# p2 as three fp32r products instead of one plain fp32 product, with a12 split into a high and a low part, in 33 of 41 groups of the SwiGLU layers

## The chip, the core and the metric

One core of one Trainium2 chip runs the whole program. The metric is the device time of one execution in microseconds (us). TensorE (PE) multiplies, VectorE (DVE), ScalarE (ACT) and GpSimd (POOL) work on elements, and SyncE (SP) issues the loads of the weights.

## The reference, cut to what matters

Two layers, each of them x += 0.5 SwiGLU(norm x); x += Mixer(norm x); x += 0.5 SwiGLU(norm x), on 528 positions (16 learned ones and 512 given ones) of 1024 features, in float32. The four SwiGLU stages are what the change touches:

```
def swiglu(h, w_gate, w_up, w_down):
    return (jax.nn.silu(h @ w_gate) * (h @ w_up)) @ w_down
h = h + 0.5 * swiglu(rmsnorm(h, g[0]), ffn_w_gate[layer, 0], ffn_w_up[layer, 0], ffn_w_down[layer, 0])
```

w_gate and w_up are 1024 x 2816 (22 tiles of 128 columns each), w_down is 2816 x 1024. The last stage needs the 512 given positions alone.

## The kernel before

**Tiles and precision.** Positions lie along the free axis, features along the 128 partitions. A float32 number is split into a high part, rounded to the type fp32r (ACT writes it, into `wh` for weights, `fh` and `hs` for activations), and a low part, the rest (DVE subtracts, into `wl`, `fl`, `hs`). A product of 128x128 weights with a block of columns is then three matmuls in fp32r: high by high, high weights by low activations, low weights by high activations. One product, p2, is not split: it multiplies the float32 `raw` and `ff` as they are, one matmul call for each 128x128 block, and each call shows in the trace as two matmul instructions.

**Passes and groups.** Each of the four stages q is two passes p (10 and 12 hidden tiles of 128; the first six tiles of the first stage are done in the ordinary way). A pass works through groups g of two hidden tiles, a and b, with the gate's and the up projection's weights side by side: 2, 6, 5, 6, 5, 6, 5 and 6 groups, 41 in all. Within a group the 2x2 blocks (input features in two halves, positions in two halves of 264, or 256 in the last stage) are multiplied by Strassen's method in Winograd's form: seven products p1 to p7, for the gate (n = 2g) and for the up projection (n = 2g+1). Each product has four 128x128 blocks, so it is 12 fp32r matmuls, and p2 is 8 records of the plain kind. The weights' quarters a11, a21, a22, a12 of 128x1024 are loaded by SP into the four slots of `raw`; DVE and ACT make the sums s1 to s4 and the parts of them. p2 is a12 by B21 (the second feature half, first positions half), added to p1 in the same bank of PSUM; s4 is a12 + s2.

**The order.** Each engine follows an order written out by hand in the program, and waits on semaphores. In the leading group of a pass (`leads(g)`) PE does p1 p5 of the gate, p1 p5 of up, p2, p2, p6, p6, p7, p7, p4, p3, p3, p4. In each later one, here with a dash for up: p1, p7, (p3' of the group before), p6, (p4' of the group before), p2, p5, p1', p7', p3, p6', p4, p2', p5'. The parts in brackets are there from the pass's third group on, which is called a steady group here; the pass's second group is without them. In a steady group DVE does c22, `low_s2`, `low_s1`, then `up_a_out` and `sum_s4` (both wait for p3' of the group before), `hidden_low` and further work. ACT does `high_s1`, `p1_copy`, `hidden_high`, `u_copy`, `high_s4` and further work. p5 adds to a bank that `u_copy` fills with p6's result. SP loads a11 of the next group when `sum_s4` is done, a12 of the next group when both p2 are done.

After its groups each pass does its part of the down projection (`down`): 8 output tiles, each from two chunks of `w_down` of 5 or 6 blocks (640 or 768 columns) in slots 1024 wide; the conversions of a chunk cover all 1024 columns. During the last output tiles ACT and DVE prepare the quarters of the next pass's leading group.

GpSimd clears `ss` seven times, copies and multiplies in the two mixers, and does nothing in the groups.

Of the kernel before, what the change touches and what calls it, by code (L numbers as in the profile page):

```python
# [5 lines left out]
F32R = mybir.dt.float32r  # L6
# [79 lines left out]
def leads(g):  # L86

    return g == GROUP[PASS_OF[g]][0]


def leading(g):
# [93 lines left out]
def trunk(nc, x_dram, gains, w_gu, w_dn, ev_in, ev_out, od_in, od_out, conv_w, sinks, rel_bias, gate_b, pool_w,  # L185
          pool_scale, ident_in, onehot_in, causal_in, sel_in, out):
    table_dram = nc.dram_tensor("bias_table", [P, 8, TABLE], F32, kind="Internal").ap()
    with ExitStack() as ctx:
        def sb(name, shape, dt=F32):
            return ctx.enter_context(nc.sbuf_tensor(name, shape, dt))  # L190
# [3 lines left out]


        x = sb("x", [P, KT, L])
        raw = sb("raw", [P, RING, CW])
        wh_at = (nc.sbuf_base + 31) // 32 * 32
        wh = sb("wh", [P, 6, CW], F32R)
        wl_at = (nc.sbuf_base + 31) // 32 * 32  # L200
# [4 lines left out]
        up = sb("up", [P, L])  # L205
        ss = sb("ss", [P, L])
        sq = sb("sq", [P, L])
        spare_at = (nc.sbuf_base + 31) // 32 * 32
        spare = sb("spare", [P, 3, L + 2])
        sb("spare_end", [P, 8])  # L210
        ss_parts = nc.alloc_sbuf_tensor_at("ss_parts", [P, 2, L], F32R, offset=spare_at + (4 * (L + 2) + 31) // 32 * 32)
        gate2, up2 = spare[:, 0, 2:2 + L], spare[:, 1, 0:L]
        ones_r = sb("ones_r", [P, P], F32R)
# [149 lines left out]
        form_ready, first_ready, u_added = sem("form_ready"), sem("first_ready"), sem("u_added")  # L363
        down_front, down_back, down_scaled = sem("down_front"), sem("down_back"), sem("down_scaled")
        table_kept = sem("table_kept")

        block = ctx.enter_context(nc.Block())

# [36 lines left out]
            return ss_parts[:, part, :]  # L405
        def gain(v, m):
            return g_sb[:, bass.ds(KT * v + m, 1)]

        def raw_quarter(kind, g):
            return raw[:, raw_slot(kind, g), :]  # L410
# [135 lines left out]
        def _(act):  # L546
            def high(n):

                slot = n % RING
                act.wait_ge(raw_in[slot], RAW_COUNT[n])  # L550
                for (q, p), (first, count) in GROUP.items():
                    at = n - CHUNK[down_name(q, p)]
                    if 0 <= at < RING:
                        form = (p6_done, p5_done, p3_done, p4_done)[at]
                        act.wait_ge(form, 2 * (first + count))
                if n >= RING:
                    act.wait_ge(chunk_done, n - RING + 1)
                act.activation(wh[:, slot, :], raw[:, slot, :], ACT.Copy).then_inc(wh_ready, 1)  # L558

            def next_high(n):  # L560
                if n + RING < CHUNKS:
# [52 lines left out]
            def high_a22(g):  # L614
                ring_done("a22", g)
                act.wait_ge(raw_in[raw_slot("a22", g)], RAW_COUNT["a22", g])
                if g:
                    act.wait_ge(p4_done, 2 * g)
                act.activation(wh[:, form_slot("a22", g), :], raw_quarter("a22", g), ACT.Copy).then_inc(a22_high, 1)

            def split_x(v, m, to):
                act.activation(to[:, m, 0, :], x[:, m, :], ACT.Copy, scale=gain(v, m)).then_inc(xh_ready, 1)
# [82 lines left out]
            def groups(q, p):  # L705
                real = q == 3
                lo = N_META if real else 0
                first, count = GROUP[q, p]
                end = first + count
                for g in range(first, end):  # L710
                    if g > first:
                        high_s1(g)
                        p1_copy(2 * g, real)
                    if g == first:
                        p1_copy(2 * g + 1, real)
                        high_a22(g)
                        high_a11(g + 1)
                        if q and not p:
                            pair_root(V_FFN[q], real)
                            warm(ACT.Silu)  # L720
                    if g > first:
                        hidden_high(g - 1, real, 0)
                        u_copy(2 * g, real)
                        high_s4(g)
                        high_a22(g)
                        hidden_high(g - 1, real, 1)
                    if g == first:
                        u_negative(2 * g, real)
                        if (q, p) == (0, 0):
                            act.wait_ge(hl_ready, STD_F)  # L730
                        u_negative(2 * g + 1, real)
                    p7_copy(2 * g, real)
                    if g > first:
                        u_negative(2 * g, real)
                        p1_copy(2 * g + 1, real)
                    if g > first and g + 1 < end:
                        high_a11(g + 1)
                    if g + 1 < end:
                        high_s3(g + 1)
                    if g > first:  # L740
                        u_copy(2 * g + 1, real)
                        act.wait_ge(hl_ready, FT * q + group_f(g))
                    p7_copy(2 * g + 1, real)
                    if g > first:
                        u_negative(2 * g + 1, real)
                    if g + 1 == end:
# [12 lines left out]
                hidden_high(end - 1, real, 1)  # L759
                high(n + 2)  # L760
                high(n + 3)
# [13 lines left out]
            def down(q, p):  # L775
# [8 lines left out]
                for i in range(KT):  # L784
# [27 lines left out]
                    if g is not None and i == 7:  # L812
                        p1_copy(2 * g, real)
                        high_s4(g)
                    if x_next:
                        x_high(q + 1, i, False)
                    if g is not None and i == 5:
# [251 lines left out]
        def _(pool):  # L1069
# [8 lines left out]
            def clear_ss(v):  # L1078
# [6 lines left out]
            clear_ss(1)  # L1085

            pool.memset(zbuf[:, 0:2], 0.0).then_inc(pool_step, 1)
            steps[0] += 1
# [19 lines left out]
                    pool.tensor_tensor(zbuf[:, 2:2 + L], conv_c[:, :], conv_x[:, :], ALU.mult).then_inc(z_ready, 1)  # L1108
            clear_ss(2)
            clear_ss(3)  # L1110
            clear_ss(4)

            for s in range(OD_TILES):
                if s == 0:
# [27 lines left out]
            pool.wait_ge(yd_l, 4)  # L1142
            clear_ss(5)
            clear_ss(6)
            pool.wait_ge(x_gained, KT - 1)
            for h, (a, b) in enumerate(ENDS):
                pool.wait_ge(rms_ready, 7 + h)
# [5 lines left out]
        def _(dve):  # L1153
# [8 lines left out]
            def low(n):  # L1162

                slot = n % RING
                dve.wait_ge(wh_ready, n + 1)
                dve.tensor_tensor(wl[:, slot, :], raw[:, slot, :], f32(wh[:, slot, :]), ALU.subtract).then_inc(wl_ready, 1)  # L1166

            def low_gates(n):

# [80 lines left out]
            def low_a22(g):  # L1250
                slot = form_slot("a22", g)
                dve.wait_ge(a22_high, g + 1)
                dve.tensor_tensor(wl[:, slot, :], raw_quarter("a22", g), f32(wh[:, slot, :]), ALU.subtract).then_inc(a22_low, 1)

            def add_square(v, i, real=False):

# [157 lines left out]
            def groups(q, p):  # L1414
# [4 lines left out]
                for g in range(first, end):  # L1419
# [20 lines left out]
                        c22(2 * g - 1, real)  # L1440
                    low_s2(g)
                    low_s1(g)
                    up_a_out(g - 1, real)
                    sum_s4(g)
                    hidden_low(g - 1, real, 0)
                    if g > first + 1:
                        c21(2 * g - 1, real)
# [14 lines left out]
                        low(n)  # L1462
                    c21(2 * g, real)
                    gate_b_scale(g, real)
                c22(2 * end - 1, real)
                low(n + 1)
                up_a_out(end - 1, real)
# [7 lines left out]
            def down(q, p):  # L1475
# [6 lines left out]
                for i, m in enumerate(order):  # L1482
# [30 lines left out]
                        low_s1(g)  # L1513
                    if g is not None and i == 7:
                        low_s4(g)
                    if x_next:
                        x_low(q + 1, i, False)
                    if g is not None and i == 5:
# [417 lines left out]
        def _(pe):  # L1936
# [116 lines left out]
            def p2(n, real, q=None):  # L2053
                s, g = n % 2, n // 2
                w, slot = width(real), raw_slot("a12", g)
                pe.wait_ge(raw_in[slot], RAW_COUNT["a12", g])
                pe.wait_ge(p1_copied, n + 1)
# [28 lines left out]
            def ffn(q, p):  # L2086
# [4 lines left out]
                for g in range(first, end):  # L2091
# [428 lines left out]
```

## Time and profile before

| | |
|---|---|
| median of 3 runs | 1844.7 us (1844.44 to 1845.2) |
| the profiled execution: device time | 1844.85 us |
| its span, first to last instruction | 1843.0 us |
| mean granted TensorE clock | 0.998 of 2.4 GHz |
| PE busy | 1822.8 us, 99% of the span |
| DVE busy | 1347.9 us, 73% |
| ACT busy | 867.3 us, 47% |
| POOL busy | 53.2 us, 3% |
| PE's share of the chain that ended last | 94% |

Busy time is the time in which an engine has an instruction under way. Matmuls overlap in the records: one lasts longer than the step from its start to the next start, and the steps are what add up to the time. In the chain that ended last, each piece is given its step.

### The profile page before, as it was taken

The page shows a single profiled execution, that of the slowest core. Times are in us where ns is not written, and L with a number is a line of the kernel's source. Part 1 is how long each engine was busy: PE and PEld are TensorE (multiplying, and loading weights), DVE is VectorE, ACT ScalarE, POOL GpSimd, SP SyncE. Part 2 cuts the span into 40 slices and gives each one's busy share as a digit, 9 for nine tenths or more (in the row PEclk, how much of TensorE's full clock was granted, in tenths as well). Part 3 has the DMA queues.
Part 4 walks back from the last instruction along what each step waited for, and adds up shares of the span by engine and source line. Part 5 has one row for each costly group of instructions (what it writes and reads, how often), then busy time and mean ns, then how long its engine had stood idle before and what let it go on. Part 6 is the DMA issues. An engine that isn't in the chain of part 4 may idle for free.

```text
span 1843.0 us, 32078 instructions
## 1 busy us (share of the span) xinstructions
PE 1822.8 (99%) x13192; PEld 1724.7 (94%) x13192; DVE 1347.9 (73%) x1777; ACT 867.3 (47%) x1367; POOL 53.2 (3%) x68
## 2 busy tenths in 40 slices
PE   8999999999999999999999999999999999999997
PEld 8999999999999999999999999999998899889986
DVE  7767787657678867886888678865656798678855
ACT  7443554434445543554555335544422555435542
POOL 0000000000000000000000000000123000000000
PEclk9999999999999999999999999999999999999999
DMA  5255233341222333233223332333212222332331
GB/s 177 88 90 115 94 114 101 106 134 59 69 70 81 104 93 114 81 104 103 81 92 106 94 99 92 109 104 118 92 58 69 69 82 102 101 105 93 109 105 62
DMA packets 81104, 176.83 MB, mean 96 GB/s; under 512 B 7292, under 2 KB 12700, under 8 KB 80960
## 3 DMA queue, kind: packets, MB, share of 16 engines
q1 hardware_dynamic: 80544, 174.49, 30.6%
q8 instruction: 106, 1.74, 0.4%
q14 instruction: 38, 0.31, 0.1%
q10 hardware_dynamic: 416, 0.29, 0.0%
HBM read 171.35 MB, written 3.41 MB: 95 GB/s over the span
## 4 chain that ended last, share of the span: by engine, by line
PE 94%; DVE 2%; ACT 1%; issue 1%; DMA 0%; SPq 0%; DVEq 0%; ACTq 0%
PE psum L1944 25%; PE psum L2014 13%; PE psum L2016 12%; PE psum L2017 12%; PE psum L2061 8%; PE psum L1954 7%; PE psum L1953 4%; PE psum L1957 4%; PE psum L1952 4%; PE psum L1956 3%; ACT wh L608 0%; DMA rb_sb<-in_rel_bias 0%; DVE rms L1319 0%; PE psum L2228 0%; DVE wl L1166 0%
## 5 line engine op out<-in xcount | busy, mean ns | idle before, releaser
L2014 PE MATMUL psum<-fh,wh 128*128 128x264 f32 (+1 forms) x1968 | 572.0, 291 | 2.5 <-ACT psum L673 2.5
L2017 PE MATMUL psum<-fh,wl 128*128 128x264 f32 (+1 forms) x1968 | 557.2, 283 | 0.0
L2016 PE MATMUL psum<-fl,wh 128*128 128x264 f32 (+1 forms) x1968 | 556.9, 283 | 0.0
L2014 PEld LDWEIGHTS psum<-fh,wh 128*128 128x128 f32 x1968 | 371.1, 189 | 6.4 <-issue 4.0
L2016 PEld LDWEIGHTS psum<-fl,wh 128*128 128x128 f32 x1968 | 371.0, 189 | 2.4
L2017 PEld LDWEIGHTS psum<-fh,wl 128*128 128x128 f32 x1968 | 369.9, 188 | 0.0
L1166 DVE TENSOR_TENSOR wl<-raw,wh 128x1024 fp32r<-128x1024 f32 x193 | 237.4, 1238 | 95.7 <-ACT wh L558 95.2
L558 ACT ACTIVATE wh<-raw 128x1024 fp32r<-128x1024 f32 x194 | 203.2, 1055 | 210.8 <-PE psum L1944 165.6
L1944 PE MATMUL psum<-xs,wh 128*128 128x264 f32 (+1 forms) x1504 | 267.3, 297 | 5.8 <-DVE xs L1269 4.2
L1944 PEld LDWEIGHTS psum<-xs,wh 128*128 128x128 f32 x1504 | 213.6, 189 | 16.5 <-issue 5.3
L1954 PE MATMUL psum<-hs,wh 128*128 128x512 f32 x528 | 206.6, 391 | 0.0
L1944 PE MATMUL psum<-hs,wh 128*128 128x512 f32 (+2 forms) x760 | 192.3, 349 | 0.0
L1944 PE MATMUL psum<-xs,wl 128*128 128x264 f32 (+1 forms) x736 | 161.9, 294 | 0.0
L2061 PE MATMUL psum<-ff,raw 128*128 128x264 f32 (+1 forms) x656 | 156.7, 384 | 0.0
L1953 PE MATMUL psum<-hs,wh 128*128 128x272 f32 x528 | 152.5, 289 | 0.0
L1957 PE MATMUL psum<-hs,wl 128*128 128x272 f32 x528 | 151.3, 287 | 0.0
L1952 PE MATMUL psum<-hs,wh 128*128 128x272 f32 x528 | 150.6, 285 | 0.0
L1956 PE MATMUL psum<-hs,wl 128*128 128x256 f32 x528 | 147.6, 280 | 0.0
L1944 PEld LDWEIGHTS psum<-hs,wh 128*128 128x128 f32 x760 | 128.4, 188 | 20.0
L2061 PEld LDWEIGHTS psum<-ff,raw 128*128 128x128 f32 x656 | 119.1, 189 | 15.8
L1944 PE MATMUL psum<-hs,wl 128*128 128x512 f32 (+2 forms) x380 | 122.8, 351 | 0.0
L1957 PEld LDWEIGHTS psum<-hs,wl 128*128 128x128 f32 x528 | 99.1, 188 | 22.0
(298 smaller groups left out, 2707.4 us busy)
## 6 DMA issues: line engine op xcount, KB each, us to landing
raw<-in_w_gate_up SPq DMA_DIRECT2D x175, 512.0 KB, 3.6
raw<-in_w_down SPq DMA_DIRECT2D x64, 384.0 KB, 3.2
raw<-in_w_down SPq DMA_DIRECT2D x64, 320.0 KB, 3.0
raw<-in_od_in SPq DMA_DIRECT2D x21, 512.0 KB, 3.5
raw<-in_ev_in SPq DMA_DIRECT2D x18, 512.0 KB, 3.5
raw<-in_ev_out SPq DMA_DIRECT2D x8, 512.0 KB, 3.5
raw<-in_od_out SPq DMA_DIRECT2D x8, 512.0 KB, 3.4
x<-in_x_t SPq DMA_DIRECT2D x8, 264.0 KB, 5.6
```

Of the source, the lines that this page charges most:

```text
L558: act.activation(wh[:, slot, :], raw[:, slot, :], ACT.Copy).then_inc(wh_ready, 1)
L1166: dve.tensor_tensor(wl[:, slot, :], raw[:, slot, :], f32(wh[:, slot, :]), ALU.subtract).then_inc(wl_ready, 1)
L1944: last = pe.matmul(dst, weights[:, slot, w], both[:, at, part, tok], start=start and p == 0, stop=stop and p == len(steps) - 1)
L1952: pe.matmul(a, wh[:, slot, w], both[:, k, 0, 0:FRONT], start=start, stop=False)
L1953: pe.matmul(a, wh[:, slot, w], both[:, k, 1, 0:FRONT], start=False, stop=False)
L1954: pe.matmul(psum[:, 2 * acc_at + 1, :].rearrange("p (h t) -> p h t", h=2), wh[:, slot, w], both[:, k, :, b], start=start, stop=False, skip ...
L1956: pe.matmul(back(acc_at, 0), wl[:, slot, w], both[:, k, 0, b], start=False, stop=stop, skip_group_check=True)
L1957: return pe.matmul(a, wl[:, slot, w], both[:, k, 0, 0:FRONT], start=False, stop=stop)
L2014: pe.matmul(psum[:, bank, 0:w], wh[:, slot, cols], high_x, start=start and j == 0, stop=False, skip_group_check=True)
L2016: pe.matmul(psum[:, bank, 0:w], wh[:, slot, cols], low_x, start=False, stop=False, skip_group_check=True)
L2017: last = pe.matmul(psum[:, bank, 0:w], wl[:, slot, cols], high_x, start=False, stop=j == 3, skip_group_check=True)
L2061: last = pe.matmul(psum[:, 4 * s, 0:w], raw[:, slot, 512 * s + P * j:512 * s + P * (j + 1)], ff[:, B21, j, 0:w], start=False, stop=j == 3, ...
```

## The change

p2 is split like the others in every group but the first two of each p = 0 pass: 41 - 8 = 33 groups by the program's own rule `plain(g)`. (The change was described as 35 groups, 31 of them with GpSimd; the program's rules give 33 and 29.) For it:

- ACT rounds a12 to fp32r (`high_a12`) into memory taken from `spare`, `sq` and `up`.
- The low part is written over a12 in `raw`, by GpSimd in the 29 groups that do not lead a pass, by DVE in the 4 leading groups of the p = 1 passes. It waits for `sum_s4`, which still reads a12.
- B21 is split once for each stage: ACT and DVE (`high_b21`, `low_b21`) write into `fl`.
- DVE's `sum_s4` is moved ahead of `up_a_out` in the steady groups.
- PE's order changes in the second group of each p = 1 pass: p1, p7, p6, p5, p1', p7', p2, p3, p6', p4, p2', p5'.
- The conversions of the down projection's chunks cover only the columns in use.

The `low_a12` and `groups` shown with `pool` are GpSimd's; DVE's `low_a12` subtracts in the same way.

```diff
+def plain(g):
+    q, p = PASS_OF[g]
+    return p == 0 and g < GROUP[q, p][0] + 2
+def parted(g):
+    return sum(not plain(h) for h in range(g + 1))
...
+            def high_a12(g):
+                q, p = PASS_OF[g]
+                act.wait_ge(raw_in[raw_slot("a12", g)], RAW_COUNT["a12", g])
+                act.wait_ge(p2_done, 2 * g)
...
+                act.activation(a12_in(g)[:, :], raw_quarter("a12", g), ACT.Copy).then_inc(a12_split, 1)
+            def high_b21(q, real):
+                act.wait_ge(t_ready, 4 * q + 4)
+                act.activation(fl[:, B12, :, 0:w], ff[:, B21, :, 0:w], ACT.Copy).then_inc(b21_split, 1)
...
                     if g > first:
+                        if not plain(g):
+                            high_a12(g)
                         hidden_high(g - 1, real, 0)
                         u_copy(2 * g, real)
                         high_s4(g)
...
+            def low_a12(g):
+                pool.wait_ge(a12_split, 2 * parted(g) - 1)
+                pool.wait_ge(s4_sum, g + 1)
+                pool.tensor_tensor(raw_low[:, raw_slot("a12", g), :], raw_quarter("a12", g), f32(a12_in(g)[:, :]),
+                                   ALU.subtract).then_inc(a12_split, 1)
+            def groups(q, p):
+                first, count = GROUP[q, p]
+                for g in range(first + 1, first + count):
+                    if not plain(g):
+                        low_a12(g)
...
+                w = chunk_cols(n)
+                dve.tensor_tensor(wl[:, slot, 0:w], raw[:, slot, 0:w], f32(wh[:, slot, 0:w]), ALU.subtract).then_inc(wl_ready, 1)
...
                     low_s2(g)
                     low_s1(g)
-                    up_a_out(g - 1, real)
+                    if g == first + 1:
+                        up_a_out(g - 1, real)
                     sum_s4(g)
+                    if g > first + 1:
+                        up_a_out(g - 1, real)
                     hidden_low(g - 1, real, 0)
...
+                    if q and not p and g == first + 1:
+                        low_b21(q, real)
...
                     if g is not None and i == 7:
                         low_s4(g)
+                        if not p:
+                            low_a12(g)
...
             def p2(n, real, q=None):
+                pe.wait_ge(p1_copied, n + 1)
+                if not plain(g):
+                    pe.wait_ge(b21_split, 2 * PASS_OF[g][0] + 2)
+                    pe.wait_ge(a12_split, 2 * parted(g))
+                    for j in range(4):
+                        cols = slice(512 * s + P * j, 512 * s + P * (j + 1))
+                        high_x, low_x = fl[:, B12, j, 0:w], fl[:, B21, j, 0:w]
+                        pe.matmul(psum[:, 4 * s, 0:w], a12_in(g)[:, cols], high_x, start=False, stop=False, skip_group_check=True)
+                        pe.matmul(psum[:, 4 * s, 0:w], a12_in(g)[:, cols], low_x, start=False, stop=False, skip_group_check=True)
+                        last = pe.matmul(psum[:, 4 * s, 0:w], raw_low[:, slot, cols], high_x, start=False, stop=j == 3,
+                                         skip_group_check=True)
+                    last.then_inc(p2_done, 1)
+                    return
...
+                    if p and g == first + 1:
+                        p6(n, real)
+                        p5(n, real)
+                        p1(n + 1, real)
+                        p7(n + 1, real)
+                        p2(n, real)
+                        p3(n, real)
+                        p6(n + 1, real)
+                        p4(n, real)
+                        p2(n + 1, real)
+                        p5(n + 1, real)
+                        continue
```

## Rows read from the trace of the kernel before

**Rows 1.** The page: busy time by engine, and the plain p2 among the groups.

```profile
PE 1822.8 (99%) x13192; PEld 1724.7 (94%) x13192; DVE 1347.9 (73%) x1777; ACT 867.3 (47%) x1367; POOL 53.2 (3%) x68
...
L2061 PE MATMUL psum<-ff,raw 128*128 128x264 f32 (+1 forms) x656 | 156.7, 384 | 0.0
...
raw<-in_w_gate_up SPq DMA_DIRECT2D x175, 512.0 KB, 3.6
```

**Rows 2.** The waits of PE: total us, times, longest.

```profile
PE psum L2014 <- ACT psum L673: 2.5, 8, 0.3
```

**Rows 3.** The chain that ended last, 723 to 790 us: start, us, engine, line.

```profile
730.11 3.56 PE psum L2061 x16
...
750.24 1.78 PE psum L2061 x8
...
760.75 1.78 PE psum L2061 x8
...
771.26 1.78 PE psum L2061 x8
```

**Rows 4.** The same chain in the last stage, 256 columns wide.

```profile
1646.01 3.45 PE psum L2061 x16
...
1696.48 1.73 PE psum L2061 x8
1706.75 1.73 PE psum L2061 x8
```

**Rows 5.** Timeline of DVE, a steady group that began at 764.0 us.

```profile
768.37 0.71 DVE L1389 TENSOR_TENSOR up<-psum,gate 128x528 f32<-128x528 f32 x1 [1.10 <-PE psum L2017]
768.99 1.22 DVE L1243 TENSOR_TENSOR ws<-raw 128x1024 f32<-128x1024 f32 x1
...
777.35 1.23 DVE L1185 TENSOR_TENSOR wl<-raw,wh 128x1024 fp32r<-128x1024 f32 x1 [1.19 <-ACT wh L583]
```

**Rows 6.** Timeline of ACT and of SP's queue, the same group.

```profile
765.92 0.37 ACT L673 ACTIVATE psum<-psum 128x264 f32<-128x264 f32 x1
...
769.11 0.65 ACT L703 ACTIVATE hs<-up 128x528 fp32r<-128x528 f32 x1 [2.82 <-DVE up L1389]
```
```profile
762.61 21.38 SPq L456 DMA_DIRECT2D raw<-in_w_gate_up  x5
```

**Rows 7.** Timeline of DVE and GpSimd in the odd mixer.

```profile
1328.68 0.71 DVE L1324 TENSOR_TENSOR gate<-psum,rms 128x528 f32<-128x528 f32 x1 [2.13 <-PE psum L1944]
1329.47 1.07 POOL L1134 TENSOR_TENSOR spare<-gate 128x527 f32<-128x527 f32 x1 [0.47 <-DVE gate L1324]
1329.83 1.79 DVE L1166 TENSOR_TENSOR wl<-raw,wh 128x1024 fp32r<-128x1024 f32 x1 [0.45 <-ACT wh L558]
```

**Rows 8.** GpSimd's subtraction and its smallest multiplication, by line: ns min/median/max.

```profile
L1140 POOL TENSOR_TENSOR up<-up,gate x2: 1283/1284/1286, 1333.1 to 1402.4; 128x512 f32<-128x512 f32 x2
```
```profile
L1149 POOL TENSOR_TENSOR x<-x,rms x4: 717/798/964, 1831.7 to 1838.4; 128x256 f32<-128x256 f32 x4
```

**Rows 9.** Timeline, PE's restart after a wait for ACT.

```profile
747.94 0.28 PE L2017 MATMUL psum<-fh,wl 128*128 128x264 f32 x1
748.01 0.37 ACT L673 ACTIVATE psum<-psum 128x264 f32<-128x264 f32 x1
...
748.52 0.36 PE L2014 MATMUL psum<-fh,wh 128*128 128x264 f32 x1 [0.31 <-ACT psum L673]
...
748.72 0.28 PE L2016 MATMUL psum<-fl,wh 128*128 128x264 f32 x1
```

**Rows 10.** Timelines of leading groups: ACT, DVE, and DVE in the last stage.

```profile
727.56 1.06 ACT L612 ACTIVATE wh<-ws 128x1024 fp32r<-128x1024 f32 x1 [1.40 <-DVE ws L1243]
```
```profile
728.65 1.23 DVE L1248 TENSOR_TENSOR wl<-ws,wh 128x1024 fp32r<-128x1024 f32 x1 [1.12 <-ACT wh L612]
```
```profile
1644.08 1.23 DVE L1248 TENSOR_TENSOR wl<-ws,wh 128x1024 fp32r<-128x1024 f32 x1 [1.13 <-ACT wh L612]
```

**Rows 11.** Timeline of ACT in the second group of a p = 1 pass.

```profile
750.01 0.65 ACT L703 ACTIVATE hs<-up 128x528 fp32r<-128x528 f32 x1 [1.63 <-DVE up L1389]
750.57 0.37 ACT L680 ACTIVATE psum<-psum 128x264 f32<-128x264 f32 x1
```

More of the change, by code:

```diff
@@ L88, in leads, with chunk_cols @@
     return g == GROUP[PASS_OF[g]][0]
+def chunk_cols(n):
+    for q in range(4):
+        for p in range(2):
+            if CHUNK[down_name(q, p)] <= n < CHUNK[down_name(q, p)] + COUNT[down_name(q, p)]:
+                return PASS_F[p] // 2 * P
+    return CW
+def plain(g):
[3 more added lines that the diff above has]
+    return sum(not plain(h) for h in range(g + 1))
 def leading(g):
@@ L196, in trunk @@
         x = sb("x", [P, KT, L])
+        raw_at = (nc.sbuf_base + 31) // 32 * 32
         raw = sb("raw", [P, RING, CW])
+        raw_low = nc.alloc_sbuf_tensor_at("raw_low", [P, RING, CW], F32R, offset=raw_at)
         wh_at = (nc.sbuf_base + 31) // 32 * 32
@@ L210, in trunk @@
         sb("spare_end", [P, 8])
+        sq_at = (nc.sbuf_base + 31) // 32 * 32
+        sq = sb("sq", [P, L])
+        up = sb("up", [P, L])
+        high_12 = nc.alloc_sbuf_tensor_at("high_12", [P, CW], F32R, offset=spare_at + (8 * (L + 2) + 31) // 32 * 32)
+        first_12 = nc.alloc_sbuf_tensor_at("first_12", [P, CW], F32R, offset=sq_at)
         ss_parts = nc.alloc_sbuf_tensor_at("ss_parts", [P, 2, L], F32R, offset=spare_at + (4 * (L + 2) + 31) // 32 * 32)
@@ L365, in trunk @@
         table_kept = sem("table_kept")
+        a12_split, b21_split = sem("a12_split"), sem("b21_split")
         block = ctx.enter_context(nc.Block())
@@ L407, in gain, with a12_in @@
             return g_sb[:, bass.ds(KT * v + m, 1)]
+        def a12_in(g):
+            return first_12 if leads(g) else high_12
         def raw_quarter(kind, g):
@@ L557, in high @@
                     act.wait_ge(chunk_done, n - RING + 1)
-                act.activation(wh[:, slot, :], raw[:, slot, :], ACT.Copy).then_inc(wh_ready, 1)
+                w = chunk_cols(n)
+                act.activation(wh[:, slot, 0:w], raw[:, slot, 0:w], ACT.Copy).then_inc(wh_ready, 1)
             def next_high(n):
@@ L745, in groups @@
                         u_negative(2 * g + 1, real)
+                    if q and not p and g == first + 1:
+                        high_b21(q, real)
                     if g + 1 == end:
@@ L814, in down @@
                         high_s4(g)
+                        if not p:
+                            high_a12(g)
+                    if (q, p) == (0, 0) and i == 1:
+                        high_b21(0, False)
                     if x_next:
@@ L1082, in clear_ss @@
                 pool.wait_ge(ss_zero, v + 1)
+            def low_a12(g):
[8 more added lines that the diff above has]
+                        low_a12(g)
             clear_ss(0)
             clear_ss(1)
+            groups(0, 1)
             pool.memset(zbuf[:, 0:2], 0.0).then_inc(pool_step, 1)
@@ L1110, in _ @@
             clear_ss(3)
+            groups(1, 0)
+            groups(1, 1)
             clear_ss(4)
+            groups(2, 0)
+            groups(2, 1)
             for s in range(OD_TILES):
@@ L1144, in _ @@
             clear_ss(6)
+            groups(3, 0)
+            groups(3, 1)
             pool.wait_ge(x_gained, KT - 1)
@@ L1165, in low @@
                 dve.wait_ge(wh_ready, n + 1)
-                dve.tensor_tensor(wl[:, slot, :], raw[:, slot, :], f32(wh[:, slot, :]), ALU.subtract).then_inc(wl_ready, 1)
+                w = chunk_cols(n)
+                dve.tensor_tensor(wl[:, slot, 0:w], raw[:, slot, 0:w], f32(wh[:, slot, 0:w]), ALU.subtract).then_inc(wl_ready, 1)
             def low_gates(n):
@@ L1253, in low_a22, with low_a12, low_b21 @@
                 dve.tensor_tensor(wl[:, slot, :], raw_quarter("a22", g), f32(wh[:, slot, :]), ALU.subtract).then_inc(a22_low, 1)
+            def low_a12(g):
+                dve.wait_ge(a12_split, 2 * parted(g) - 1)
+                dve.tensor_tensor(raw_low[:, raw_slot("a12", g), :], raw_quarter("a12", g), f32(a12_in(g)[:, :]),
+                                  ALU.subtract).then_inc(a12_split, 1)
+            def low_b21(q, real):
+                w = width(real)
+                dve.wait_ge(b21_split, 2 * q + 1)
+                dve.wait_ge(p2_done, 2 * GROUP[q, 0][0] + 4)
+                dve.tensor_tensor(fl[:, B21, :, 0:w], ff[:, B21, :, 0:w], f32(fl[:, B12, :, 0:w]), ALU.subtract).then_inc(b21_split, 1)
             def add_square(v, i, real=False):
@@ L1464, in groups @@
                     gate_b_scale(g, real)
+                    if q and not p and g == first + 1:
+                        low_b21(q, real)
                 c22(2 * end - 1, real)
@@ L1515, in down @@
                         low_s4(g)
+                        if not p:
+                            low_a12(g)
+                    if (q, p) == (0, 0) and i == 2:
+                        low_b21(0, False)
                     if x_next:
```

10 lines of the change are left out of this document (7 added, 3 removed).

## The prediction

> **What bounds the kernel now.** I read the page's busy times first: PE has an instruction under way in 99% of the span, DVE in 73%, and GpSimd in 3% [rows 1]. Then the waits of PE: in the groups the only one is for a copy of ACT's, 8 times and 2.5 us in all [rows 2]. So the groups are paced by PE's own steps, and two things can move the time there: fewer or cheaper steps, and waits that are new.
>
> The chain that ended last gives the steps. A plain p2 is 8 records and 1.78 us with 264 columns [rows 3], 1.73 us with 256 [rows 4]. Between the end of one p2 (762.53) and the start of the next (771.26) lie six split products: 8.73 / 6 = 1.455 us for one [rows 3]. With 256 columns it is (10.27 - 1.73) / 6 = 1.423 us [rows 4].
>
> **What the change gives.** A split p2 has the same 12 matmuls as any other product, so I price it at 1.455 and 1.423 us. 33 groups have two p2 each. 24 of them are in the first three stages: 48 x (1.78 - 1.455) = 15.6 us. 9 are in the last: 18 x (1.73 - 1.423) = 5.5 us. The gain is 21.1 us, all of it on the path that bounds.
>
> **The new wait in the steady groups.** There are 25 with GpSimd: 18 with 264 columns (4 in the first stage's second pass, 3 + 4 in each of the next two) and 7 with 256. Before, p2 needed only a12 in its slot. Now it needs a chain that begins when p3' of the group before ends, because `sum_s4` waits for that, and GpSimd overwrites what `sum_s4` reads. Step by step, from the moment PE leaves p3':
>
> - DVE starts 0.02 us later: p3' ends two products before p2, at 771.26 - 2.91 = 768.35, and DVE's next instruction starts at 768.37 after 1.10 us of idling [rows 3, 5]. That instruction is `up_a_out` now; `sum_s4`, behind it at 768.99, is the first one after the change. It takes 1.22 us [rows 5].
> - GpSimd starts 0.08 us after DVE has ended: 1328.68 + 0.71 = 1329.39, against 1329.47 [rows 7].
> - Its subtraction of 128x1024 is nowhere in this trace. The nearest row is the same operation with 512 columns, 1284 ns; the smallest, undisturbed instruction with 256 took 717 ns [rows 8]. The line through both gives 1284 + 2 x 567 = 2418 ns. From below I take the addition of 527 columns, 1.07 us [rows 7], scaled by 1024/527: 2.08 us. From above, twice 1284: 2.57 us. I take 2.40, near the line, since it rests on the same operation.
> - PE restarts 0.22 us after the event: ACT ended at 748.38, and the second matmul of the product started at 748.72, which is one step of 0.12 after an effective start of 748.60 [rows 9].
>
> The Trainium skill ("GPSIMD Engine Reference", section "Performance versus the Vector engine") gives 4497 ns for a two-input fp32 operation on 2048 columns and calls about 2.6 cycles for an element the floor. Half of it would be 2.25 us, an estimate from that page; by it the sum below would be 3.8 us smaller. The rows with 512 columns are a little slower than that, and I go by the rows.
>
> The chain is 0.02 + 1.22 + 0.08 + 2.40 + 0.22 = 3.94 us. What covers it is p6 and p4' on PE, 2.91 us, or 2.85 with 256 columns. So p2 starts 1.03 or 1.09 us late: 18 x 1.03 + 7 x 1.09 = 26.1 us. PE executes in order, so nothing fills that time.
>
> ACT's part of the split does not gate: `p1_copy` ends at 766.3, the a12 load is issued at 762.61 and lands some 3.6 us later, at 766.2 [rows 1, 6], so `high_a12` is over by 767.4, two us before `sum_s4`. It stands ahead of `hidden_high`, which started at 769.11 after 2.82 us of idling and now waits for the moved `up_a_out` [rows 6]; `u_copy` follows at about 771, and p5 needs it only after p2.
>
> **The leading groups of the p = 1 passes.** PE reaches p2 at 730.11 [rows 3]. ACT ends `high_s4` at 728.62 and `high_a12` at 729.6; DVE ends `low_s4` at 729.88, and its `low_a12` at 1.14 us later, the step of two such instructions [rows 10]: about 731.0. With 0.22 for the restart p2 starts at 731.2, 1.1 us late. The groups of three stages lie alike: 3.4 us. In the last stage `low_s4` ends at 1645.31, `low_a12` at 1646.45, and p2 was due at 1646.01 [rows 4, 10]: 0.66 us. Together 4.0 us; bounds 0 (if the split can come earlier) and 6.
>
> **The second groups of the p = 1 passes.** Their new order puts p5 straight behind p6, and p5 adds to the bank that `u_copy` fills from p6. Until now p2 covered that copy. p6 ends where p2 began, at 750.24; the copy ran from 750.57, behind `hidden_high`, to 750.94 [rows 3, 11]. With 0.22 for the restart p5 starts at 751.16: 0.92 us, four times, 3.7 us. GpSimd is in time there: p2 comes three products later, at about 755.5, and `sum_s4` is over by 751.2. What it may cost beyond that is c22 arriving late behind the held-up work of DVE: 0 to 1 us, taken as 0.
>
> **What costs nothing.** 33 roundings of a12 on ACT are hidden by its idle time (47% busy). B21's split is about one more instruction each on ACT and DVE, in each stage: in the second group of a p = 0 pass it comes just ahead of c22 and `low_s2`, and DVE idles 1.10 us right before `up_a_out` in that stretch [rows 5]. If that cover were gone it would cost up to 1.2 us three times. The narrower conversions take work from DVE and ACT during the down projections, while PE is busy anyway [rows 1], so I give them nothing. SP's load of a11 is released by `sum_s4` 0.6 us earlier in relation to p3', that of a12 as before.
>
> DVE loses time too while GpSimd works. A DVE instruction with two SBUF inputs that started at 1329.83, beside GpSimd's of 1329.47 to 1330.54, took 1.79 us and not 1.22, as if it had waited to its end [rows 7]. Here `hidden_low` will wait so, about 1 us. The cover is the 1.19 us for which DVE idled before `low_a11` [rows 5], and two us more in which the next group's forms are ahead of PE. The Trainium skill ("SBUF — State Buffer", section "SBUF: two separate sides") calls the shared port pair an exclusive lock held for the whole instruction; the rows agree as far as one pair can.
>
> **The sum.** -21.1 + 26.1 + 4.0 + 3.7 = +12.7 us. The profiled execution took 1844.85 us (0.15 above the median), so 1857.5 there and 1857.4 against the median of 1844.7: 0.7% slower. The point of balance is a GpSimd instruction of 2.40 - 12.7 / 25 = 1.89 us, below my lower bound; at 2.08 the sum is +4.7, at 2.57 it is +17.
>
> **The rivals.**
>
> 1. GpSimd's chain doesn't hold PE up. For it: the stall hangs on an instruction that this trace does not show. Against it: the instruction would have to end within 1.37 us, and half the columns take 1.28. With only the leading and second groups' waits the time is 1844.7 - 21.1 + 7.7 = 1831; with none at all 1824. It decides as soon as GpSimd takes clearly under 1.89 us, or if the wait for p3' comes earlier than I read it. Chance 0.20.
> 2. Stall and gain cancel: GpSimd at 1.9 to 2.0 us, or at 2.08 with the leading and second groups' waits half hidden (+0.8). 1841 to 1848. Chance 0.12.
> 3. GpSimd also waits for DVE. An instruction of DVE's with two SBUF inputs gets the port first and GpSimd starts behind it, 0.6 to 1.2 us later. Against it: behind `sum_s4` comes `up_a_out`, which reads PSUM, and after it ACT must first finish `hidden_high`. The time is 1857 + 25 x 0.6 = 1872 or more. Chance 0.08.
> 4. My forecast, 1848 to 1866: chance 0.60.
>
> **Range and chances.** From case 4's bounds I go down through the balance and half of rival 1, and a little up: 1831 to 1868. Within 0.2% (3.7 us, about what a measurement of this kernel can tell from no change) 0.11. Faster 0.23: rival 1 and a part of 2. Slower 0.66.
>
> **What the profile after would show.** PE's waits would name a new row, p2's first matmul waiting for GpSimd's subtraction, about 25 times and about 1 us each (by the record some 0.2 less). GpSimd's instruction lasts about 2.4 us. In the chain GpSimd and `sum_s4` have a share of 25 x 3.6 us, about 5%, where PE's falls. The step from one p2 to the next in a steady stretch grows from 10.51 us by about 0.2 on the mean. p2 shows 12 steps of 0.12 us. I am wrong if GpSimd's instruction is under 1.9 us, if `sum_s4` starts before p3' has ended, or if PE's busy share stays at 99%.

## The result, and the profile after

The changed kernel takes 1868.0 us (median of 4 runs, 1867.81 to 1868.86) against 1844.95 us, a ratio of 1.0126 (95% interval 1.0112 to 1.0139): 23 us slower. Forecast were 12.7 us, 1857.4 us, with a range that ended at 1868, which the measured 1868.01 us just misses. The direction was right, and so were most of the places where time is lost; the forecast loss is little more than half of the measured one.

The page of the changed kernel, against [rows 1]. TensorE (PE) has fallen from 99% to 97% of the span:

```profile
span 1866.1 us, 32745 instructions
...
PE 1812.2 (97%) x13456; PEld 1723.9 (92%) x13456; DVE 1348.1 (72%) x1785; ACT 863.0 (46%) x1404; POOL 123.3 (7%) x97
...
PE 82%; DVE 8%; POOL 3%; issue 2%; ACT 2%; DMA 2%; SPq 0%; DVEq 0%; POOLq 0%; ACTq 0%
...
L1143 POOL TENSOR_TENSOR raw_low<-raw,high 128x1024 fp32r<-128x1024 f32 x29 | 70.2, 2422 | 1002.2 <-DVE ws L1319 1002.2
```

PE's share of the chain that ended last went from 94% to 82%, and GpSimd's subtraction (L1143), 2.42 us each, stands in it with DVE's `sum_s4` (L1319). The waits of PE, where [rows 2] stood alone among the groups before (a wait under 0.15 us is not in this list):

```profile
PE psum L2160 <- POOL raw_low L1143: 27.0, 25, 1.3
PE psum L2160 <- DVE raw_low L1333: 3.7, 4, 1.1
PE psum L2111 <- ACT psum L728: 3.4, 4, 0.9
PE psum L2111 <- ACT psum L721: 2.5, 8, 0.3
...
PE psum L2111 <- DVE spare L1468: 1.5, 3, 0.8
```

The first is p2 waiting for GpSimd, 25 times: one for each steady group. Its recorded mean is 1.08 us; the time lost is larger, as the group below shows. The second is p2 in the four leading groups, the third p5 behind `u_copy` in the four second groups. The last one, c22 coming late, is new too; the prediction named it and took it as 0. A steady group, by the timelines of PE, DVE and POOL; before, DVE did `up_a_out` first [rows 5]:

```profile
797.41 0.28 PE L2114 MATMUL psum<-fh,wl 128*128 128x264 f32 x1
797.53 0.28 PE L2111 MATMUL psum<-fh,wh 128*128 128x264 f32 x1
...
801.64 0.36 PE L2160 MATMUL psum<-fl,high 128*128 128x264 f32 x1 [1.02 <-POOL raw_low L1143]
801.84 0.28 PE L2161 MATMUL psum<-fl,high 128*128 128x264 f32 x1
...
803.20 0.28 PE L2111 MATMUL psum<-fh,wh 128*128 128x264 f32 x1
```
```profile
797.73 1.23 DVE L1319 TENSOR_TENSOR ws<-raw 128x1024 f32<-128x1024 f32 x1 [1.26 <-PE psum L2114]
798.87 0.70 DVE L1477 TENSOR_TENSOR up<-psum,gate 128x528 f32<-128x528 f32 x1
800.29 1.77 DVE L1500 TENSOR_TENSOR hs<-up,hs 128x528 fp32r<-128x528 f32 x1 [0.71 <-ACT hs L751]
```
```profile
799.10 2.39 POOL L1143 TENSOR_TENSOR raw_low<-raw,high 128x1024 fp32r<-128x1024 f32 x1 [19.28 <-DVE ws L1319]
```

PE leaves p3' at 797.53, where p6's first matmul starts. DVE starts `sum_s4` 0.20 us later and ends at 798.96, GpSimd runs from 799.10 to 801.49, and PE goes on at an effective 801.72 (one step of 0.12 before its second matmul). That is 4.19 us, where p6 and p4' cover 24 steps of 0.122, 2.93 us. So p2 starts 1.26 us late. `hidden_low` (L1500), which has two inputs in SBUF, takes 1.77 us in place of 0.70: it ends at 802.06, 0.57 us after GpSimd, as if it had begun its work only when GpSimd was done.

I put the starts of all p2 in both timelines side by side. From p2 to p2' the changed kernel is 0.22 to 0.24 us faster, from p2' to the next group's p2 mostly 0.87 to 0.93 us slower. The whole ledger, in us:

| term | forecast | measured |
|---|---|---|
| 66 cheaper p2 | -21.1 | -19.6 |
| steady groups, 25 waits | +26.1 | +31.2 |
| leading groups of p = 1, 4 waits | +4.0 | +4.7 |
| second groups of p = 1, 4 waits | +3.7 | +4.2 |
| third groups behind these | 0 (0 to 1) | +3.3 |
| B21's split, 3 places | 0 | +0.3 |
| start of the execution | none | -1.0 |
| sum | +12.7 | +23.1 (spans 1866.1 and 1843.0) |

How the measured column comes about: the gain from the experiment on it (below). Leading groups: from the last p2' of the pass before to their first p2 the changed kernel is 1.22, 0.91, 0.92 and 0.42 us slower, to which come the cheaper p2' that lies between (0.30, in three of them) and 0.08 because the first matmul after a wait is recorded that much early. Second groups: from the first p2 of the pass to their p2' 0.23 to 0.26 each, plus three cheaper p2, less the 0.08, since here the stretch begins at a matmul that is recorded early. Third groups: their step from p2' to p2 is longer by 1.50, 1.89, 2.15 and 1.32, where 0.88 (0.93 in the last stage) is usual. B21's split: the same step in the third groups of the p = 0 passes, less what is usual there. Steady groups: what is left, 1.25 us each, which agrees with the 1.26 read from the single group above. The start is no effect of the change: up to the first p2 the executions of this study took 87.3 to 88.8 us, depending on how soon the first x tiles land (4.5 us for one after, 5.6 before).

### The profile page after: what moved, and what is told of

The parts are those of the page before. It is cut to its first block, busy times and chain, and to the rows that moved or that the text cites. A ratio compares the mean times of both kernels' runs of the same rounds, so it can differ in the third digit from the quotient of the medians.

```text
span 1866.1 us, 32745 instructions
## 1 busy us (share of the span) xinstructions
PE 1812.2 (97%) x13456; PEld 1723.9 (92%) x13456; DVE 1348.1 (72%) x1785; ACT 863.0 (46%) x1404; POOL 123.3 (7%) x97
## 3 DMA queue, kind: packets, MB, share of 16 engines
q8 instruction: 108, 1.77, 0.4%
## 4 chain that ended last, share of the span: by engine, by line
PE 82%; DVE 8%; POOL 3%; issue 2%; ACT 2%; DMA 2%; SPq 0%; DVEq 0%; POOLq 0%; ACTq 0%
PE psum L2041 25%; PE psum L2111 9%; PE psum L2113 9%; PE psum L2114 9%; PE psum L2051 7%; PE psum L2050 4%; PE psum L2054 4%; PE psum L2049 3%; PE psum L2053 3%; POOL raw_low L1143 3%; DVE ws L1319 2%; PE psum L2160 2%; PE psum L2161 2%; PE psum L2162 2%; PE psum L2170 1%
## 5 line engine op out<-in xcount | busy, mean ns | idle before, releaser
L2111 PE MATMUL psum<-fh,wh 128*128 128x264 f32 (+1 forms) x1968 | 561.1, 285 | 7.4 <-ACT psum L728 3.4
L588 ACT ACTIVATE wh<-raw 128x1024 fp32r<-128x1024 f32 (+2 forms) x194 | 169.2, 879 | 224.7 <-PE psum L2041 172.8
L1242 DVE TENSOR_TENSOR wl<-raw,wh 128x1024 fp32r<-128x1024 f32 (+2 forms) x193 | 194.8, 1016 | 95.8 <-ACT wh L588 95.4
L1143 POOL TENSOR_TENSOR raw_low<-raw,high 128x1024 fp32r<-128x1024 f32 x29 | 70.2, 2422 | 1002.2 <-DVE ws L1319 1002.2
L2041 PEld LDWEIGHTS psum<-xs,wl 128*128 128x128 f32 x736 | 116.8, 188 | 2.7
```

Of the source, the lines that this page charges most:

```text
L588: act.activation(wh[:, slot, 0:w], raw[:, slot, 0:w], ACT.Copy).then_inc(wh_ready, 1)
L1143: pool.tensor_tensor(raw_low[:, raw_slot("a12", g), :], raw_quarter("a12", g), f32(a12_in(g)[:, :]), ALU.subtract).then_inc(a12_split, 1)
L1242: dve.tensor_tensor(wl[:, slot, 0:w], raw[:, slot, 0:w], f32(wh[:, slot, 0:w]), ALU.subtract).then_inc(wl_ready, 1)
L2041: last = pe.matmul(dst, weights[:, slot, w], both[:, at, part, tok], start=start and p == 0, stop=stop and p == len(steps) - 1)
L2111: pe.matmul(psum[:, bank, 0:w], wh[:, slot, cols], high_x, start=start and j == 0, stop=False, skip_group_check=True)
```

## Experiments

Each edit is to the changed kernel, unless another is named. Those executed more than once have a ratio to the kernel before, which ran beside them at 1844.2 to 1844.4 us.

**The low part on VectorE.** GpSimd's loop is empty, and DVE has

```diff
                     sum_s4(g)
+                    if not plain(g) and not pooled_low(g):
+                        low_a12(g)
                     if g > first + 1:
                         up_a_out(g - 1, real)
```

> The changed kernel, with the low part of a12 made by VectorE right behind sum_s4 in all 33 groups; GpSimd makes none. Theory (the chain p3', sum_s4, GpSimd's subtraction sets the start of p2 in the steady groups): the chain becomes 0.20 + 1.23 + 1.14 + 0.23 = 2.80 us against the 2.93 us that p6 and p4' cover, so the 25 waits of some 1.2 us go (-31 us), and with them what GpSimd's hold on the port costs behind the second groups (-3): 1834 us, with the waits of the leading groups left. Rival (VectorE is too full for 29 more instructions of 1.14 us): the waits for GpSimd are replaced by waits of PE for VectorE's other work (c22, low_s2), and the time is 1845 to 1868.

Measured: 1834.06 us, ratio 0.9944 (0.9929 to 0.9959). The waits for GpSimd are gone and none of DVE's took their place; those of the leading and second groups are as they were:

```profile
PE psum L2168 <- DVE raw_low L1339: 3.7, 4, 1.1
PE psum L2119 <- ACT psum L734: 3.4, 4, 0.9
PE psum L2119 <- ACT psum L727: 2.5, 8, 0.3
```

The chain through GpSimd is the cause of the loss, and DVE, the busiest engine behind PE, still had room for 29 more instructions of 1.14 us. The spans of the two kernels differ by 33.6 us; the ledger has 31.2 + 3.3 for the steady and third groups. The rest of the ledger without the start, -19.6 + 4.7 + 4.2 + 0.3 = -10.4 us, is close to the measured -10.2.

**Half of GpSimd's work.**

```diff
-pool.tensor_tensor(raw_low[:, raw_slot("a12", g), :], raw_quarter("a12", g), f32(a12_in(g)[:, :]), ...)
+pool.tensor_tensor(raw_low[:, raw_slot("a12", g), 0:CW // 2], raw_quarter("a12", g)[:, 0:CW // 2], f32(a12_in(g)[:, 0:CW // 2]), ...)
...
+                        low_cols = cols if leads(g) else slice(P * j, P * (j + 1))
```

> The changed kernel, where GpSimd subtracts only the first 512 of 1024 columns in its 29 groups, and p2' of the up projection takes its low weights from the gate's half: it leaves out the up projection's low part of a12. Theory (the duration of GpSimd's instruction is in the chain one for one): the instruction falls from 2.42 to about 1.28 us, as the one on 512 columns in the mixer, and the waits from 1.08 us each to about 0.1: 1838 us. Rival (the wait is a fixed cost of handing over between engines, or hangs on sum_s4 alone): over 1860 us.

Measured: 1837.9 us (one execution). GpSimd's instruction took 1.33 us on the mean (1.30 in the steady groups), and PE's list has one wait for it:

```profile
L1143 POOL TENSOR_TENSOR raw_low<-raw,high 128x512 fp32r<-128x512 f32 x29 | 38.6, 1332 | 1003.4 <-DVE ws L1319 1003.4
```
```profile
PE psum L2160 <- POOL raw_low L1143: 0.4, 1, 0.4
```

The list leaves out what is under 0.15 us. Side by side with the first experiment, where the wait is gone, p2 is still some 0.17 us late in each steady group, and the chain with 1.30 us for GpSimd gives the same: 0.20 + 1.23 + 0.14 + 1.30 + 0.23 = 3.10 us against 2.93. So 1.09 us less of GpSimd's instruction took about 1.08 us from every wait: its length is in the chain one for one, and the rival is out. The extra 3.3 us of the third groups went as well.

**GpSimd apart from sum_s4.** The wait that could be taken away by giving the result a place of its own:

```diff
+low_12 = nc.alloc_sbuf_tensor_at("low_12", [P, CW], F32R, offset=hs_at + PASS_F[0] * 2 * row)
...
 pool.wait_ge(a12_split, 2 * parted(g) - 1)
-pool.wait_ge(s4_sum, g + 1)
-pool.tensor_tensor(raw_low[:, raw_slot("a12", g), :], raw_quarter("a12", g), ...)
+pool.tensor_tensor(low_12[:, :], raw_quarter("a12", g), ...)
...
+                        low_w = raw_low[:, slot, cols] if leads(g) else low_12[:, cols]
```

> The changed kernel, where GpSimd writes the low part of a12 into memory of its own (the place of the hidden tiles 10 and 11, not in use during the groups) and so need not wait for sum_s4. Theory: GpSimd starts when high_a12 ends, 1.2 us before p3' ends, and is done 1.4 us before p2 is due, so PE waits for it nowhere in the steady groups: -31 us, 1837 us. sum_s4 has two inputs in SBUF and waits for GpSimd's end instead, some 1.3 us, which the forms' lead over PE covers. Rival (that hold on VectorE is not covered): PE waits for VectorE instead, 25 times 0.5 us or more, 1850 us or more.

Measured: 1854.0 us, ratio 1.0054 (1.0039 to 1.0069). My expectation fell and the rival held: the edit more than halves the loss, and does not end it. Two groups of it, DVE and GpSimd:

```profile
794.22 3.22 DVE L1319 TENSOR_TENSOR ws<-raw 128x1024 f32<-128x1024 f32 x1 [1.26 <-PE psum L2114]
...
815.47 1.23 DVE L1319 TENSOR_TENSOR ws<-raw 128x1024 f32<-128x1024 f32 x1
```
```profile
793.96 2.40 POOL L1143 TENSOR_TENSOR low<-raw,high 128x1024 fp32r<-128x1024 f32 x1 [17.65 <-ACT high L662]
815.56 3.39 POOL L1143 TENSOR_TENSOR low<-raw,high 128x1024 fp32r<-128x1024 f32 x1 [19.20 <-ACT high L662]
```

Where GpSimd came first (793.96 to 796.36), `sum_s4` took 3.22 us in place of 1.23 and ended at 797.44, 1.08 us after GpSimd. Where `sum_s4` came first (815.47 to 816.70), GpSimd took 3.39 us in place of 2.40 and ended at 818.95, 2.25 us after it. The recorded times overlap, but the second of the two ended each time about its own length, less 0.15 us, after the first: it did its work when the first was done. So PE waits in either case, once for `u_copy`, which stands on ACT behind `hidden_high` and that behind DVE, once for GpSimd:

```profile
PE psum L2111 <- ACT psum L729: 12.8, 18, 1.0
PE psum L2160 <- POOL low L1143: 6.3, 7, 1.0
```

18 + 7 are the 25 steady groups. This is what the Trainium skill says ("SBUF — State Buffer", section "SBUF: two separate sides"): whichever of a VectorE operation with two SBUF inputs and a GpSimd operation starts first has the port for its whole instruction. The rows agree, with 3.22 and 3.39 us.

**The gain alone.** From the kernel before; p2 takes the place, shape and number of a split product, on operands that lie ready:

```diff
+if not (PASS_OF[g][1] == 0 and g < GROUP[PASS_OF[g]][0] + 2):
+    pe.wait_ge(s2_low if leads(g) else s1_low, g + 1)
+    product(wh, form_slot("s2" if leads(g) else "s1", g), s, T1, 4 * s, False, real, q).then_inc(p2_done, 1)
+    return
```

> The kernel before, with nothing changed but p2 in the 33 groups: 12 fp32r matmuls in place of the 8 plain records, on operands that lie ready for another product (s1's parts and T1, in leading groups s2's parts), with no new conversion and no new wait. It leaves out a12 by B21. It measures the gain alone. By the steps of the trace after (1.78 less 1.48 us at 264 columns, 0.29 at 256) -19.6 us: 1825 us. By the prediction's 1.455 us for a product -21.1 us: 1824 us. If splitting as such gives much less on the path, 1835 us or more.

Measured: 1824.67 us against 1844.28, ratio 0.9893 (0.9876 to 0.9909): -19.6 us for 66 p2, 0.297 each. A split p2 of 264 columns is 1.48 us in the timeline after (803.20 less 801.72), not 1.455; with 256 columns it is 1.42, as forecast.

**sum_s4 behind up_a_out again.**

```diff
-                    if g == first + 1:
-                        up_a_out(g - 1, real)
+                    up_a_out(g - 1, real)
                     sum_s4(g)
-                    if g > first + 1:
-                        up_a_out(g - 1, real)
```

> The changed kernel, with sum_s4 behind up_a_out again in the steady groups, as in the kernel before. Theory (the chain from p3' through sum_s4 and GpSimd sets p2's start): every steady group's wait grows by up_a_out's step of 0.62 us, 25 x 0.62 = 15.5: 1883.5 us. Rival (p2 waits for GpSimd's port or its duration alone, sum_s4's place does not matter): 1868 us.

Measured: 1922.5 us (one execution), +54.5 and not +15.5. The waits for GpSimd grew from 27.0 to 50.2 us, by 0.93 each: 0.62 for `up_a_out`, and 0.3 because `hidden_low` now holds the port when GpSimd comes (its instruction takes 2.69 us). The other 31 us are TensorE's clock. Behind 20 of the 25 waits the step from p2 to p2' is 1.5 us longer than in the changed kernel, and the granted clock falls there, each time for 3.4 us; behind the other 5 neither happens, though their gaps were as long. The windows around one such wait, whose columns are the stretch, its length, the busy time and number of instructions of each engine, the granted clock, the DMA share and GB/s:

```profile
819.00:821.20 2.20, 0.33 (x3) 0.11 (x1) 1.73 (x2) 1.43 (x2) 2.11 (x1) 1.00 0.58 168
821.20:824.00 2.80, 2.74 (x14) 2.77 (x15) 2.23 (x3) 1.20 (x3) 0.00 (x0) 0.60 0.63 243
824.00:827.00 3.00, 3.00 (x22) 3.00 (x21) 0.95 (x2) 0.00 (x0) 0.00 (x0) 0.81 0.00 0
827.00:830.00 3.00, 3.00 (x27) 3.00 (x26) 1.79 (x3) 1.34 (x2) 0.00 (x0) 1.00 0.32 91
```
```profile
821.70 0.38 PE L2157 MATMUL psum<-fl,high 128*128 128x264 f32 x1
821.87 0.42 PE L2158 MATMUL psum<-fl,high 128*128 128x264 f32 x1
822.09 0.42 PE L2159 MATMUL psum<-fl,raw_low 128*128 128x264 f32 x1
```

PE issued nothing from 819.16 to 821.26. From 821.8 to 824.95 its step is 0.22 us and not 0.12: the lower of the two levels, 1.2 GHz. That costs about 1.5 us more, 20 times. What sets the 5 waits without it apart stays open. The direction (the chain through `sum_s4` sets p2's start) was right, and the size was off for a reason that neither theory had.

**The old order in the second groups.** TensorE's special order there is taken out.

```diff
-                    if p and g == first + 1:
-                        p6(n, real)
-                        p5(n, real)
...
-                        continue
```

> The changed kernel, with TensorE's order in the second groups of the p = 1 passes as before (p1, p7, p6, p2, p5, ...). Theory: there the wait of p5 for u_copy goes (-1.1 us each), and p2 waits for GpSimd's end instead, which lies 4.0 us after p2's turn; part of what followed in the third groups goes: +2 to +2.9 us in each of four groups, 1876 to 1880 us. Rival (the new order costs more than it saves): under 1868 us.

Measured: 1884.1 us (one execution), +16.1. p2 now waits for GpSimd in these groups too, once in each for 3.85 us or so:

```profile
PE psum L2160 <- POOL raw_low L1143: 41.8, 29, 3.9
```

and the mean granted clock fell from 0.998 to 0.993. The time lies above the theory's 1880 us, and the clock accounts for that: at each of the four gaps, 4.1 us from one matmul's start to the next, it went to the lower level, twice for 6.8 us and twice for 3.4. Some 16.7 us of matmul work ran at that level, and half of it, 8 us, is an estimate of what that cost. The other 8 us, 2.0 for each group, are the lower end of what the theory said. The new order is worth keeping with GpSimd, though it brings p5's wait.

**VectorE in the second groups only.** `pooled_low(g)` is false for `g == first + 1`, so that DVE makes the low part in these four and GpSimd in the 25 steady groups.

> The changed kernel, with VectorE in place of GpSimd for the low part in the four second groups of the p = 1 passes alone. Theory (there GpSimd's hold on the port makes up_b_gate last 2.8 us, low_a22 and so the load of the next a22 come late, and PE waits in the third group): the extra 0.6, 1.0, 1.3 and 0.4 us of the third groups go, -3.3: 1864.7 us. Rival (these come from the 1.14 us more of ACT's or DVE's work, high_a12 and the like, whoever subtracts): 1868 us.

Measured: 1865.66 us, ratio 1.0116 (1.0099 to 1.0133), 2.35 us less than the changed kernel. The waits for L1468 have gone from PE's list. In the changed kernel, the second group of a pass:

```profile
757.21 0.70 DVE L1500 TENSOR_TENSOR hs<-up,hs 128x528 fp32r<-128x528 f32 x1
757.83 2.92 DVE L1488 TENSOR_TENSOR spare<-spare 128x528 f32<-128x528 f32 x1
...
762.76 1.21 DVE L1329 TENSOR_TENSOR wl<-raw,wh 128x1024 fp32r<-128x1024 f32 x1
...
768.57 1.23 DVE L1286 TENSOR_TENSOR raw<-raw 128x1024 f32<-128x1024 f32 x1 [1.71 <-DMA raw<-in_w_gate_up]
```

GpSimd holds the port from 757.43, `up_b_gate` (L1488) takes 2.92 us, `low_a22` (L1329) ends late, at 764.0, and with it SP's load of the next a22, for which `sum_s1` (L1286) then waits until 768.57. The forms of the third group are late by that, and PE waits for c22 (L1468). With DVE in these groups `up_b_gate` takes 0.70 us. By the starts of p2 the third groups are shorter by 0.60, 1.01, 1.27 and 0.40 us, the ledger's 3.3 in full; in two other groups of the profiled execution p2 comes 0.3 us later than in the changed kernel's, for a reason that stays open, and the medians differ by 2.35.

**VectorE everywhere, and two products exchanged.** From the first experiment's kernel:

```diff
-                        p2(n, real, new)
-                        p2(n + 1, real, new)
+                        if not p:
+                            p2(n, real, new)
+                            p2(n + 1, real, new)
...
                         p6(n, real, new)
                         p6(n + 1, real, new)
+                        if p:
+                            p2(n, real, new)
+                            p2(n + 1, real, new)
...
                         p6(n, real)
+                        p1(n + 1, real)
                         p5(n, real)
-                        p1(n + 1, real)
                         p7(n + 1, real)
```

> VectorE makes all low parts, as in the first experiment (1834 us), and TensorE has two products exchanged: in the second groups of the p = 1 passes p1' stands between p6 and p5, in the leading groups of those passes both p2 stand behind both p6. Theory: u_copy and the leading groups' low_a12 are covered by a product each: -1.2 x 4 and -1.3 x 3 - 0.8, 1824.5 us, faster than both kernels. Rival (what is gained there is given back at the next wait, c22 or p1_copy of these groups): 1829 to 1834 us.

Measured: 1829.03 us, ratio 0.9914 (0.9900 to 0.9929). It beats both kernels, by less than I expected: the time is the lowest that the rival allowed. The waits for `low_a12` and `u_copy` (3.7 + 3.4 us) are gone, and the leading and second groups are 8.5 us shorter. The rival is right in part: the third groups take 2.7 us of that back, with a new wait for c22 (1.3 us) in two of them. This profiled execution began 1.5 us later than the first experiment's (88.8 against 87.3 us to the first p2).

**The narrower conversions alone.** From the kernel before, with `w = chunk_cols(n)` in `high` and `low`.

> The kernel before, with the conversions of the down projection's chunks cut to the 640 or 768 columns in use, and nothing else. The prediction gave this part nothing, since PE is busy during the down projections: 1844 to 1845 us, within 0.1% of the kernel before. Rival (the shorter conversions reach the path somewhere, which would hide a part of the change's cost): 1842 us or less.

Measured: 1844.42 us, ratio 1.0001 (0.9991 to 1.0010): nothing, as forecast.

## Why the prediction was right in direction and wrong in size

The mechanism was right: p2 waits for the chain p3', `sum_s4`, GpSimd, and the wait is larger than the gain. What failed is the size of terms of the sum. The largest is the new wait in the steady groups (26.1 forecast, 31.2 measured), by its first step; the next is the third groups (nothing forecast, 3.3 measured).

**The gain** (-21.1, measured -19.6). The split p2 is 1.48 us and not 1.455 at 264 columns. That six products take 1.455 us on the mean hid that they are not all alike: in the kernel before, p6 and p4' take 2.93 us together. Why some are slower stays open.

**"DVE starts 0.02 us later": the step that failed first.** I took p3's end from the chain that ended last (771.26 less two products) and DVE's start from the timeline. The chain cuts at the modelled ends of matmuls, some 0.16 us after the timeline's starts: in the timeline of the kernel before that p2 starts at 771.10 and p6 at 768.17:

```profile
768.17 0.28 PE L2014 MATMUL psum<-fh,wh 128*128 128x264 f32 x1
...
771.10 0.38 PE L2061 MATMUL psum<-ff,raw 128*128 128x264 f32 x1
```

So DVE started 0.20 us after PE had left p3', as it does now. The same mixture stands in the leading groups (730.11, in the timeline 729.94) and in the second groups (750.24, in the timeline 750.07). Corrected by 0.17 the forecasts of single waits are 1.30 us for a leading and 1.09 us for a second group, where the ledger has 1.3 and 1.05. It is worth 33 x 0.17 = 5.6 us.

**GpSimd's instruction** was forecast at 2.40 us from the line through 256 and 512 columns, and took 2.42 on the mean and 2.39 in the groups where nothing was in its way. Half of the figure in the Trainium skill ("GPSIMD Engine Reference", section "Performance versus the Vector engine"), 2.25 us, an estimate, would have been too low. Its start after DVE is 0.14 us and not 0.08, another 1.5 us in all.

**The order of DVE and GpSimd on the port** was argued rightly for the steady groups: `up_a_out` ran beside GpSimd at its usual 0.70 us, and `hidden_low` waited to GpSimd's end (1.77 us for 0.70; about 1 us more was forecast), and no wait of PE in these groups is for DVE.

**"What it may cost beyond that is c22 arriving late: 0 to 1 us, taken as 0"** was the right mechanism with the wrong size: 3.3 us in the third groups. With DVE in GpSimd's place in the second groups these 3.3 us are gone. I had followed DVE's delay to the next use of its results, and not to the load that `low_a22` releases.

**The rivals.** GpSimd's chain holds PE up in all 25 steady groups, so the first rival is out, and so is the balance of the second. Of the third (GpSimd waits for DVE) the steady groups show nothing, 2.39 us each; in three of the second groups it took 2.7 us, and in the fourth it started 0.49 us after `sum_s4`, without harm to p2. The point of balance was said to be 1.89 us for GpSimd's instruction. By the measured sum it is 2.42 - 23.1 / 25 = 1.50 us, an estimate. The half-length run, faster than the kernel before with 1.33 us, fits both and does not decide between them.

**What the profile was to show.** PE's new waits are 25 of 1.08 us as recorded (about 1 was said, and by the record some 0.2 less), GpSimd and `sum_s4` have 3% + 2% of the chain (5%), and p2 has 12 steps of 0.12 us. From p2 to the next group's p2 it is 21.67 us against 21.01, so the step between two p2 grew by 0.33 us on the mean, not by 0.2.

**The sum.** To the 12.7 us forecast come 5.6 for the first step, 1.5 for GpSimd's later start, 3.3 for the third groups, 1.5 of gain that did not come and 0.3 for B21's split. Off go 1.0 for the start of the execution and 0.4 because p6 and p4' cover 2.93 us and not 2.91 in 18 groups. That is 23.5 us, against 23.1 measured; the 0.4 us too much are not assigned.

## What to carry to other kernels

Before work goes to an idle engine, write down the chain that it joins and what covers that chain in time: GpSimd was 97% idle, and its 2.4 us came on top of 1.8 us of other steps in a chain that only 2.9 us of matmuls cover, while VectorE, 73% busy, did the same in 1.14 us, and the waits of the steady groups were gone. A subtraction of two numbers from a trace is only as good as their common clock: take both from one view. And an instruction that is held up on an in-order engine is to be followed to the loads it releases, not only to its own readers.

## What the runs showed of the hardware

- GpSimd's instruction and a VectorE instruction with two SBUF inputs exclude each other, whichever comes first: 3.22 for 1.23 us on the one side, 3.39 for 2.40 us on the other. `up_a_out`, with one input in PSUM, took its usual 0.70 us beside GpSimd.
- Of 25 gaps of 2.1 to 2.5 us in TensorE's work, 20 were followed by 3.4 us at 1.2 GHz, a step of 0.22 us for 0.12, which cost 1.5 us each; 5 were not. None of the 25 gaps of 1.2 to 1.5 us before p2 in the changed kernel was (granted clock 1.00 right behind them).
- A wait of TensorE costs more than its record: 0.23 us from GpSimd's end to the effective start of the next matmul, and a recorded wait of 1.02 us stands for a start 1.26 us late.
